# The input projection's last 16 columns with the weights held still and 256 tokens moving

## The reference

```
mod = c_act @ mod_w[layer] + mod_b[layer]          # six rows of 1024
h = x * (1 + sc_m) + sh_m
u, q, k, v, g_out, a_low = split(h @ w_in[layer], (512, 768, 1024, 1536, 2048))   # 2064 columns
y_s5  = _s5_group(u, ...)                          # a complex linear recurrence, in chunks
# in _gla_group (gated linear attention, chunks of 64):
log_alpha = log_sigmoid(a_low @ w_alpha_up + b_alpha) / 16
bc = cumsum(log_alpha); qc * exp(bc), kc * exp(b_last - bc), scores with decay, ...
y = concat([y_s5, y_gla]) @ w_out[layer]
x = _layer_norm(alpha * x + (1 + gt_m) * y, ...)
```

## Time and profile before

| | |
|---|---|
| median of 3 runs | 2797.34 us (2791.43, 2797.34, 2807.77) |
| profiled execution | 2799.62 us |
| its span, first to last instruction | 2797.8 us |
| mean granted clock of TensorE | 0.943 of full |
| busy: PE, PEld, DVE, ACT | 91%, 73%, 74%, 52% |
| chain that ended last | PE 70%, DVE 21%, ACT 4% |

### The profile page before, as it was taken

One profiled execution on the slowest core, in us unless ns is written; L12 is line 12 of the kernel. 1 busy time (PEld: TensorE's weight loads), 2 busy tenths in 40 slices (PEclk: granted clock), 3 DMA queues, 4 the chain that ended last, 5 costly groups with the idle time before them and its releaser, 6 DMA issues.

```text
span 2797.8 us, 32539 instructions
## 1 busy us (share of the span) xinstructions
PE 2545.7 (91%) x12413; PEld 2036.8 (73%) x12413; DVE 2081.0 (74%) x2254; ACT 1461.2 (52%) x1535; POOL 18.0 (1%) x29
## 2 busy tenths in 40 slices
PE   6988689998785999999999999998888999978998
PEld 2736667777455888888888888876677887767787
DVE  6587787665766899989898998996865554775554
ACT  1221433443133777777777787774544444544543
POOL 0001000000000000000000000000000000000000
PEclk8998899998697999999999999999999999988999
DMA  7451246753132899999999999994403553503452
GB/s 244 158 179 60 91 167 248 246 211 125 47 121 76 311 357 357 356 355 356 346 361 374 372 351 359 358 353 176 127 32 105 181 183 99 195 1 106 136 182 89
DMA packets 274343, 598.14 MB, mean 214 GB/s; under 512 B 28721, under 2 KB 37247, under 8 KB 273025
## 3 DMA queue, kind: packets, MB, share of 16 engines
q1 hardware_dynamic: 252144, 580.30, 58.4%
q10 hardware_dynamic: 22034, 15.67, 2.0%
HBM read 594.87 MB, written 1.06 MB: 213 GB/s over the span
## 4 chain that ended last, share of the span: by engine, by line
PE 70%; DVE 21%; ACT 4%; issue 2%; ACTq 1%; DMA 1%; DVEq 0%; POOLq 0%
PE PS L215 67%; DVE WL L171 5%; PE PS L237 3%; DVE WF L171 2%; ACT WH L207 2%; DVE AR L171 1%; ACTq L150 1%; DVE MW L171 1%; DVE MOD L171 1%; DVE H L171 1%; DVE HF L171 1%; DVE SMALL L182 1%; DVE X L171 1%; DVE H L176 1%; DVE HTR L171 1%
## 5 line engine op out<-in xcount | busy, mean ns | idle before, releaser
L171 DVE TENSOR_TENSOR WL<-RG,WH 128x1024 fp32r<-128x1024 f32 (+1 forms) x558 | 919.3, 1648 | 373.4 <-ACT WH L207 341.0
L207 ACT ACTIVATE WH<-RG 128x1024 fp32r<-128x1024 f32 (+1 forms) x558 | 781.7, 1401 | 617.9 <-PE PS L215 559.2
L215 PE MATMUL PS<-WH,HTR 128*128 128x512 f32 (+2 forms) x2920 | 848.8, 388 | 42.0 <-DVE HTR L171 15.1
L215 PEld LDWEIGHTS PS<-WH,HTR 128*128 128x128 f32 x2920 | 552.1, 191 | 155.3 <-DVE HTR L171 16.3
L215 PE MATMUL PS<-WL,HTR 128*128 128x512 f32 (+2 forms) x1460 | 507.3, 385 | 0.9 <-DVE WL L171 0.9
L215 PE MATMUL PS<-WH,ATR 128*128 128x512 f32 x1624 | 458.7, 394 | 17.5 <-DVE WL L171 9.5
L215 PEld LDWEIGHTS PS<-WH,ATR 128*128 128x128 f32 x1624 | 306.5, 190 | 82.7 <-DVE WL L171 16.0
L215 PE MATMUL PS<-MW,HTR 128*128 128x512 f32 x1332 | 330.0, 395 | 1.2 <-DVE MW L171 0.5
L215 PEld LDWEIGHTS PS<-WL,HTR 128*128 128x128 f32 x1460 | 279.8, 192 | 55.1 <-DVE WL L171 1.8
L215 PEld LDWEIGHTS PS<-MW,HTR 128*128 128x128 f32 x1332 | 244.4, 188 | 55.6 <-DVE MW L171 7.0
L171 DVE TENSOR_TENSOR MW<-RG,MW 128x2048 fp32r<-128x2048 f32 x112 | 256.8, 2293 | 12.0 <-DVE ATR L171 0.5
(11 more groups left out here) (230 smaller groups left out, 2006.7 us busy)
## 6 DMA issues: line engine op xcount, KB each, us to landing
RG<-in_moe_w_gate SPq DMA_DIRECT2D x112, 1024.0 KB, 6.2
RG<-in_moe_w_up SPq DMA_DIRECT2D x112, 1024.0 KB, 6.4
RG<-in_moe_w_down SPq DMA_DIRECT2D x112, 1024.0 KB, 6.3
RG<-in_w_ff SPq DMA_DIRECT2D x64, 1024.0 KB, 5.1
RG<-in_mod_w SPq DMA_DIRECT2D x48, 1024.0 KB, 5.2
RG<-in_w_in SPq DMA_DIRECT2D x34, 1024.0 KB, 5.6
RG<-in_w_out SPq DMA_DIRECT2D x16, 1024.0 KB, 5.0
RG<-in_ffn_w_gate SPq DMA_DIRECT2D x14, 1024.0 KB, 5.2
```

Of the source, the lines that this page charges most:

```text
L171: return self.did(lambda: self.e.tensor_tensor(o, a, b, op))
L207: return self.did(lambda: self.e.activation(o, a, f, bias=bias, scale=scale))
L215: return self.did(lambda: self.e.matmul(o, l, r, start=start, stop=stop))
```

## The change

The fifth block is taken out of `BLOCKS1`. Behind the four blocks, `pe_w_in` now issues 24 matmuls for it: for each of the 8 chunks three, with 128 columns of the weights' tile held still (the 16 that count, and 112 that happen to lie behind them; `p.wide` is a view that is long enough) and all 256 tokens moving. The result has the 16 columns on partitions 0 to 15, already transposed, in bank 4, and is accumulated over the chunks. DVE copies it to tB at the end of `v_w_in`. ACT's and DVE's copies of 128x16, the two transposes and the copy in `v_gla` go. With one `yield` less in `pe_gla` and `v_gla`, one `g` is taken from four of the order strings, so the two gate matmuls now stand with the q and k transposes, ahead of them.

```
-BLOCKS1 = tuple((c, min(512, INC1 - c)) for c in range(0, INC1, 512))
+BLOCKS1 = tuple((c, 512) for c in range(0, 2048, 512))
...
+                p.wide = hi[:, b:], lo[:, b:]
...
         def pe_gla(pe, l):
-            for t in range(2):
-                x = pe.tr(PS[0:16, 0, tok(t)], PR1[:, t, 2048:2064], IDN)
-            x.then_inc(gla_pe, "alT")
+            pe.wait_ge(rows_in, ROWS_OF[l])
+            pe.wait_ge(gla_v, l, "alT")
+            for c in range(2):
+                x = pe.mm(PS[:, 0, c * 256:(c + 1) * 256], ST[0:16, 128 + c * 128:256 + c * 128], tB[0:16, 0, :], True, True)
+            x.then_inc(gla_pe, "al")
             for b, o, z in ((1, 512, "q"), (2, 768, "k")):
...
-            yield
-            pe.wait_ge(rows_in, ROWS_OF[l])
-            pe.wait_ge(gla_v, l, "alT")
-            for c in range(2):
-                x = pe.mm(PS[:, 0, c * 256:(c + 1) * 256], ST[0:16, 128 + c * 128:256 + c * 128], tB[0:16, 0, :], True, True)
-            x.then_inc(gla_pe, "al")
             yield
...
         def v_gla(v, l):
-            yield
-            v.wait_ge(gla_pe, l, "alT")
-            v.cp(tB[0:16, 0, :], PS[0:16, 0, 0:256]).then_inc(gla_v, "alT")
             yield
...
-        FIRST = (0, 5, 10, 16)
-        AHEAD1, AHEAD2 = (4, 4, 4, 1, 0), (4, 4, 4, 4, 2, 0)
+        FIRST = (0, 4, 8, 14)
+        AHEAD1, AHEAD2 = (4, 4, 4, 1), (4, 4, 4, 4, 2, 0)
...
         def pe_w_in(pe, l):
...
+            yield
+            p = W.of["w_in", l, 4][0]
+            pe.wait_ge(proj_a, FIRST[l] + 3)
+            pe.wait_ge(proj_v, FIRST[l] + 3)
+            pe.wait_ge(W.lo, p.los)
+            for k in range(8):
+                c = slice(k * 16, k * 16 + 128)
+                x = pe.mm3(PS[:, 4, 0:256], p.wide[0][:, c], p.wide[1][:, c], HT8[0][:, k, :], HT8[1][:, k, :], k == 0, k == 7)
+            x.then_inc(W.used)
...
         def v_w_in(v, l):
...
+            yield
+            v.wait_ge(W.used, W.of["w_in", l, 4][0].i + 1)
+            v.cp(tB[0:16, 0, :], PS[0:16, 4, 0:256]).then_inc(gla_v, "alT")
```

In the order strings of the mixers (PE and DVE, both layers) one letter goes, here PE's of layer 0:

```
-    ("mixers0", "pe"): "mmmgmgmsmsmgmmmsmmgs...
+    ("mixers0", "pe"): "mmmgmmsmsmgmmmsmmgs...
```

More of the change, by code:

```diff
@@ L388 @@
     ("mixers0", "g"): "gggggggggggggg",
-    ("mixers0", "pe"): "mmmgmgmsmsmgmmmsmmgsmggmsggmmssssssggmsggmssggsssggsssgsssssggggggggg",
-    ("mixers0", "v"): "mgsbmgbmggsbgsggssssggbggbggmgggggggmgbsgbgbmgggggsgggggsgssggsgggggggggg",
+    ("mixers0", "pe"): "mmmgmmsmsmgmmmsmmgsmggmsggmmssssssggmsggmssggsssggsssgsssssggggggggg",
+    ("mixers0", "v"): "mgsbmbmggsbgsggssssggbggbggmgggggggmgbsgbgbmgggggsgggggsgssggsgggggggggg",
     ("mixers1", "a"): "sgmssggggbbsggggggssggggggggssgmsg",
     ("mixers1", "g"): "gggggggggggggg",
-    ("mixers1", "pe"): "sggmmsmsssgmsgsgsggmgssmssmmggssssggsssggsgssggmsmggmgmgggmggsgsmm",
-    ("mixers1", "v"): "gsmbsggmgsggssssgmggmgggggmggggggsgggsgggggsgggggggggggggggssgsmgg",
+    ("mixers1", "pe"): "sgmmsmsssgmsgsgsggmgssmssmmggssssggsssggsgssggmsmggmgmgggmggsgsmm",
+    ("mixers1", "v"): "gsmbsgmgsggssssgmggmgggggmggggggsgggsgggggsgggggggggggggggssgsmgg",
     ("attention0", "a"): "ddbkcckdkcbbcdcdbcbddccbbddcbbdccbdbcbdcdckkdkkbckk",
```

## The result

| | before | with the change |
|---|---|---|
| median on one chip (runs) | 2796.15 us (7: 2789.73 to 2807.77) | 2777.45 us (7: 2774.14 to 2786.23) |
| ratio, 95% interval | | 0.9942 (0.9921 to 0.9962): 16.2 us less (10.6 to 22.1) |
| span of the profiled execution | 2797.8 us | 2775.7 us |
| mean granted clock | 0.943 | 0.951 |
| busy: PE, DVE; chain: PE, DVE | 91%, 74%; 70%, 21% | 91%, 75%; 64%, 26% |

The kernel became 0.6% faster. The forecast was 2784 us, 2775 to 2795, from a sum of 13.96 us.

What follows compares the result with a forecast made beforehand. PE was taken as the bound, busy 91% and 70% of the chain, with both narrow blocks wholly on the path. Layer 0's 5.74 us plus layer 1's 8.22 made 13.96 us off, forecast 2784 us, 8 in 10 range 2775 to 2795.

Steps and rivals of the forecast that it cites:

- The block: Last 16 projection columns, both layers: 24 matmuls 0.120 us apart; fence 3.97 us earlier in layer 0, 4.28 in layer 1.
- the longer copy: DVE's copy ahead of each layer's fence: 0.41 us for 16x256 instead of 0.17 for 128x16, +0.24 per layer.
- what would show it: List of signs: 24 records in 2.9 us, full clock at both fences, no DVE idle ahead of layer 0's first modulation row.
- The clock at the fences: Clock 1.00 from 122 to beyond 140 in layer 0, and from 686 to the end of S5's matmuls in layer 1.
- Rival 1: Layer 1's clock falls in spite of the change, behind the fence: 10.5 us gained in total, 2787 us; chance 0.23.
- Layer 0 behind the fence: DVE's idle 1.32 us and copy of 0.45 go; what comes behind 150.0 hangs on that instant and moves with it.
- the 1.32: Layer 0: DVE's 1.32 us idle, waiting for PE's first modulation row, goes because the row runs at full clock.
- the 0.45: Layer 0: the copy to tB leaves DVE's queue behind the fence, 0.41 us and 0.45 with its issue.
- Layer 1 behind the fence: At full clock DVE's stretch on HF no longer waits for PE: 3.04 + 0.90 = 3.94 us, some 18.3 behind the fence.
- The sum: Both layers: 5.74 us from layer 0 and 8.22 from layer 1, 13.96 us off the kernel.
- Rivals 2 and 3: 2: modulation weights late, gain hidden, 2793 or 2797, chance 0.10. 3: low clock through layer 0's modulation rows, 2800, chance 0.05.
- The chances: Whole kernel: 0.60 for a change within 0.5% (14 us), 0.37 for faster, 0.03 for slower.

Runs made afterwards that it cites:

- the narrow fill: The change plus 31 extra matmuls of 16 columns, results unused, ahead of the new block in each layer: 2790.36 us, ratio 0.9989 against before.

## Why the prediction was right, point by point

**The block.** 24 records at 0.119 us, predicted 0.120. The block to the fence: 3.57 and 3.56 instead of 7.66 and 7.96, so 4.09 and 4.40, predicted 3.97 and 4.28. Both are 0.12 low: I gave the longer copy 0.24 per layer, but PE's idle time at the fence went from 0.40 to 0.56, by 0.16, which explains 0.08 of it; the step of 0.119 explains 0.02. (The 2.9 us under "what would show it" don't agree with the sum's own 2.76 + 0.28 = 3.04; measured were 3.0.)

**The clock at the fences.** Full in all profiles with the new block but the one with the narrow fill ahead of it. Rival 1 fell: 16 transposes, gate matmuls with 16 rows and S5's with 32 rows held the full clock in layer 1, from 680.47 to 691.8. The rule of the Trainium skill, "TensorE: Matmul & The Clock Gate", "Part 4: PE-mode transpose", that transposes don't count as busy time like matmuls, is not confirmed here: 16 of them in two groups of 1.10 us cost nothing. They are too few to refute it. More weighs the old block in layer 1 of the kernel with layer 0 changed, where the clock rose from 0.50 to 1.00 at 693.7 behind 3.7 us of nothing but transposes; but in both executions of before 4.07 us of them did not raise it. So there the trace speaks against the page, and in before not. The page means the transposes of TensorE's transpose mode. Line 237 issues those (`self.e.transpose`, one record each, where a plain 32-bit matmul has two), and not plain 32-bit matmuls, as I wrote ahead of the prediction. S5's matmuls are no safe ground either: in layer 0 the clock fell under them in three profiles with the new block.

**Layer 0 behind the fence.** Predicted 1.32 and 0.45, 1.77 together. The idle time went, the copy went, and the second modulation row's addition stood 1.61 us nearer to the fence than in the first profile of before (18.46 instead of 20.07). HF began 2.54 us nearer: the other 0.93 are ACT's issues behind it (7.36 us before, 6.43 with the change), which I had not counted on: luck. Against the second it is -0.01. There the 1.32 didn't exist, and the 0.45 that DVE saved (its second row's addition stood 18.90 us behind the fence) was lost on ACT, whose six issues took 5.97 us in that execution and 6.43 with the change. The step that failed is my sentence that what comes behind 150.0 "hangs on that instant and moves with it": between them stand ACT's issues, whose length changes by more than the term.

**Layer 1 behind the fence.** Predicted 3.94 and HF at 18.3 us; 3.76 and 18.52 (22.28 before in both profiles; 19.37 where the low clock was short, which leaves 0.85). To the load of `s_w_glu` 4.3 us against the first profile, 2.7 against the second.

**The sum.** 13.96 predicted; the two places give 15.3 between the first two profiles, 10.7 with the second one of before (3.69 and -0.1 in layer 0, 4.36 and 2.7 in layer 1), and the runs 16.2 (10.6 to 22.1) and 12.0 (5.3 to 18.7). The 13.96 lies between these four. None of them can tell a term of one microsecond, and the agreement to 2 us is partly luck. The two blocks are sure, 7.2 to 8.5 us over all profiles of the old ones. Behind the fences 2.6 and 6.8 us more came in the two pairs of profiles, and what of that is the low clock, what ACT's issues and the spread of "load", the runs don't separate; one profile can't give it. I predicted from one.

**Rivals 2 and 3.** PE never waited for a load at either place. Low clock through both modulation rows did not come; with the narrow fill in layer 0 the clock fell, but came back within the new block (129.1), ahead of the fence.

**The chances.** I gave 0.60 to less than 0.5% and 0.37 to more. 0.58% and 0.43% were measured, on either side of that bound, which is where a sum of 14 us of 2797 belongs.

**What stays open.** Why the same narrow block kept layer 1 at half clock to 739.9 and 737.0 us in the two executions of before but to 693.7 in the kernel with layer 0 changed (where it fell again at 707.3, with PE standing still). The Trainium skill, "TensorE: Matmul & The Clock Gate", section "Part 1: The HAM clock gate (the "warmup" mystery)", says that one kernel runs a different number of matmuls cold from run to run. The rows of layer 0 in before agree (10.01 and 8.74 us for the same modulation row); a difference of 44 us goes beyond that, and more profiles of either kernel would be needed to tell chance from a cause. Nor has the new place of the gate matmuls and the copy a run of its own: the change was only tested with all its parts, one layer at a time.

## What to carry to other kernels

When a matmul with 128x128 held has few columns to move, expect it to cost as much as one with 128 (0.111 us here), and look at the granted clock in and behind it: swap the operands so that the many tokens move, or, if the layout forbids that, move more columns, up to 128, at the same pace. A term that comes from a low clock is to be priced from several executions, and one that must pass another engine's queue of DMA issues isn't worth a place in a sum under a microsecond. Work that starts earlier is a gain only as far as the next place where several engines meet: here 6.0 us at one stretch were 0.2 us at the end of the stage.

## What the runs showed of the hardware that was not expected

- A stream of matmuls with 128x128 held and 16 columns moved keeps PE and PEld busy to 2.00 of 2.00 us, and yet the granted clock goes to 0.50 in it. With 128 columns moved, and the same 0.111 us from start to start, it stays at 1.00.
- At half clock such narrow matmuls are 0.213 us apart (126.18 to 128.74 in the second execution of before, 12 steps). So what sets their pace slows with the clock.
- Matmuls with 32 rows of 32x64 held the full clock for 7.37 us in layer 1 in all twelve profiles in which they came to it, but in layer 0 it fell early under them in three of fourteen (11.6 to 11.8 us). When they came at 0.50 they did not bring it back in 13.93 us, in two profiles.
- The issue of the same six loads on ACT's queue took 5.97, 6.43, 7.36, 9.98 and 10.82 us in five executions.
